# Two gaps between arrays in SBUF resized, and 48 idle products behind the last unit

## The reference

```python
h = layer_norm(x) * (1.0 + sc1) + sh1
proj = h @ w_in
...
mix = merged @ w_out
up = causal_dwconv(h @ w_up, w_dw_f, b_dw_f)
f = (gelu(gt) * v) @ w_down
...
def swiglu(x, w13, w2):
    g, u = split(x @ w13, 2)
    return (silu(g) * u) @ w2
```

## Time and profile before

| what | value |
|---|---|
| median of 3 runs | 1039.6 us (1038.9 to 1039.86) |
| the profiled execution | 1041.34 us, span 1039.5 us |
| PE busy | 1023.4 us (98%), 7499 products |
| DVE, ACT, POOL busy | 73%, 55%, 3% |
| granted TensorE clock, mean | 0.997 |

### The profile page before, as it was taken

One profiled execution on the slowest core, in us unless ns is written; L12 is line 12 of the kernel. 1 busy time (PEld: TensorE's weight loads), 2 busy tenths in 40 slices (PEclk: granted clock), 3 DMA queues, 4 the chain that ended last, 5 costly groups with the idle time before them and its releaser, 6 DMA issues.

```text
span 1039.5 us, 18332 instructions
## 1 busy us (share of the span) xinstructions
PE 1023.4 (98%) x7499; PEld 958.9 (92%) x7499; DVE 754.0 (73%) x1293; ACT 572.9 (55%) x960; POOL 27.5 (3%) x34
## 2 busy tenths in 40 slices
PE   8999999999999999999999999999999999999997
PEld 7999998999999998999987999999899878999996
DVE  6988998899777788877867555555889576555555
ACT  5573447665555586724646445444746565444443
POOL 0000000000100042000000000000000000000000
PEclk9999999999999999999999999999999999999999
DMA  9999873588765533622245555665364426655511
GB/s 370 418 419 370 316 243 124 196 270 274 233 190 193 165 108 115 224 63 80 84 142 186 167 186 191 188 194 186 121 229 158 132 95 250 209 187 183 186 58 41
DMA packets 59603, 201.22 MB, mean 194 GB/s; under 512 B 10496, under 2 KB 10880, under 8 KB 59264
## 3 DMA queue, kind: packets, MB, share of 16 engines
q1 hardware_dynamic: 58368, 199.98, 56.2%
q10 hardware_dynamic: 1152, 0.07, 0.1%
HBM read 198.71 MB, written 1.31 MB: 192 GB/s over the span
## 4 chain that ended last, share of the span: by engine, by line
PE 86%; DVE 10%; ACT 2%; issue 1%; DMA 1%; SPq 0%; DVEq 0%; ACTq 0%
PE ps L632 73%; PE ps L1012 4%; DVE lo L1899 2%; DVE raw L1883 1%; DVE B L2356 1%; PE ps L818 1%; PE ps L720 1%; DVE B L1968 1%; PE ps L771 1%; PE ps L869 1%; DMA B<-in_t 1%; ACT hi L1300 1%; PE ps L806 0%; PE ps L791 0%; DVE sm L2180 0%
## 5 line engine op out<-in xcount | busy, mean ns | idle before, releaser
L1899 DVE TENSOR_TENSOR lo<-raw,hi 128x1024 fp32r<-128x1024 f32 x297 | 360.8, 1222 | 123.3 <-ACT hi L1300 122.6
L632 PE MATMUL ps<-hh,hi 128*128 128x256 f32 x1528 | 432.1, 283 | 2.2 <-DVE hl L1945 1.1
L632 PE MATMUL ps<-hl,hi 128*128 128x256 f32 x1528 | 426.7, 279 | 0.0
L632 PE MATMUL ps<-hh,lo 128*128 128x256 f32 x1528 | 426.7, 279 | 0.0
L1300 ACT ACTIVATE hi<-raw 128x1024 fp32r<-128x1024 f32 x305 | 318.4, 1052 | 50.2 <-PE ps L632 49.1
L632 PEld LDWEIGHTS ps<-hh,hi 128*128 128x128 f32 x1528 | 287.3, 188 | 6.3 <-issue 2.0
L632 PEld LDWEIGHTS ps<-hl,hi 128*128 128x128 f32 x1528 | 287.3, 188 | 1.9 <-issue 0.3
L632 PEld LDWEIGHTS ps<-hh,lo 128*128 128x128 f32 x1528 | 287.3, 188 | 0.0
L632 PE MATMUL ps<-hi,fh 128*128 128x512 f32 x192 | 76.3, 397 | 0.0
L632 PE MATMUL ps<-lo,fh 128*128 128x512 f32 x192 | 75.9, 395 | 0.0
L632 PE MATMUL ps<-hi,fl 128*128 128x512 f32 x192 | 75.8, 395 | 0.0
(11 more groups left out here) (333 smaller groups left out, 1277.4 us busy)
## 6 DMA issues: line engine op xcount, KB each, us to landing
raw<-in_w SPq DMA_DIRECT2D x356, 512.0 KB, 4.3
Z<-in_w SPq DMA_DIRECT2D x9, 512.0 KB, 9.9
B<-in_t SPq DMA_DIRECT2D x2, 512.0 KB, 4.9
B<-in_w SPq DMA_DIRECT2D x2, 512.0 KB, 8.5
h<-in_w SPq DMA_DIRECT2D x2, 512.0 KB, 7.7
xa<-in_x SPq DMA_DIRECT2D x1, 1024.0 KB, 8.6
B<-in_r SPq DMA_DIRECT2D x1, 1024.0 KB, 6.4
out<-h SPq DMA_DIRECT2D x4, 256.0 KB, 2.0
```

The source lines that it names most:

```text
L632: m = g.matmul(o, l, r, start=first and n == 0, stop=last and n == 2, skip_group_check=True)
L1899: g.tensor_tensor(lo[:, j % SPLIT, :], raw[:, PLACE[j] % RAW, :], hi[:, j % SPLIT, :].bitcast(F), ALU.subtract).then_inc(*up("lo", j))
```

## The change

`gap0` has 12 elements instead of 24 (48 bytes instead of 96), `gap1` 20 instead of 8 (80 instead of 32). The sum of the two is the same. In `tensor`, two helpers are defined, and the first is called four times behind the last unit: 4 x 4 x 3 = 48 narrow products into bank 4 that nobody reads, whose moving operand is `hh` or `hl` taken `shift` elements later, and whose stationary operand is slot 0 of `hi` or `lo` taken `by` elements later.

```diff
-        gap0 = sb("gap0", [P, 24])
+        gap0 = sb("gap0", [P, 12])
         hh = sb("hh", [P, NC, S], FR)
         hl = sb("hl", [P, NC, S], FR)
-        gap1 = sb("gap1", [P, 8])
+        gap1 = sb("gap1", [P, 20])
...
         def tensor(g, s):
+            def idle_rows(shift, n, by=0):
+                xh, xl = (x[:, :, :].rearrange("p a b -> p (a b)") for x in (hh, hl))
+                for k in range(n):
+                    a = k * S + shift
+                    w = k % 4 * P + by
+                    three(bank[4][:, 0:S], hi[:, 0, w:w + P], lo[:, 0, w:w + P], xh[:, a:a + S], xl[:, a:a + S], True, True)
+
+            def idle_wide(shift, n, by=0):
+                xh, xl = (x[:, :, :].rearrange("p a b -> p (a b)") for x in (hh, hl))
+                for k in range(n):
+                    a = k * S + shift
+                    three(bank[5][:, :], hi[:, 0, by:by + 512], lo[:, 0, by:by + 512], xh[:, a:a + P], xl[:, a:a + P], True, True,
+                          flip=True)
...
             ffn_tokens("w131", "w21", "w13r1", "x5", x5_free)
+            idle_rows(2, 4)
+            idle_rows(30, 4)
+            idle_rows(1, 4)
+            idle_rows(16, 4, 16)
```

## The result

The changed kernel takes 1056.4 us (median of 4 runs, 1056.38 to 1056.47) against 1039.5 us before (four runs): a ratio of 1.0165, 95% interval [1.0152, 1.0178], slower by 16.9 us. The forecast was 1055 us.

The account below looks back on a forecast made before the run. It took the time from one TensorE product's start to the next as the bound: 1041.3 us profiled + 15.3 = 1056.6, less 1.7 for the median, say 1055 us. Own range 1050 to 1058, with rival A 1025 to 1058.

Parts of the forecast that it names:

- Places: SBUF addresses: rounding to 32 bytes puts hh and hl 32 bytes nearer, not 48, and fh and all behind 32 farther.
- Part 1: 4584 narrow products moving hh or hl: 120 ns apart, the idle products' level, +15.3 us; other bound -15.3 us.
- Part 2: 528 narrow products moving fh or fl: distance 160 stays at 113.3 ns, 0 taken; bound 0 to +1.8 us.
- Part 3: Wide products, 528 over hh or hl and 576 over fh or fl: no change, bound -3.7 to +3.7 us.
- Parts 4 and 5: 48 idle products hidden under last norm and stores, cost 0; all else moved, such as transposes, 0, under +1 us.
- Sum: Whole kernel: profiled 1041.3 + 15.3 = 1056.6 us, less 1.7 for the median: 1054.9, say 1055 us.
- rival A: Operand distances repeat each 64 bytes, so hh and fh products swap levels: -13.5 us, 1026 us; chance 0.30.
- Rival B: Address doesn't matter at this grain; a phase between TensorE's two streams holds a step: 1039.6 us; chance 0.18.

Follow-up runs that it names:

- e4: Kernel before plus, behind the last unit, sets of narrow products at 64 operand distances and wide ones at 16; one execution, 113.0 to 120.0 ns at the kernels' distances.
- e12: Kernel before plus runs of 37 narrow products at 16 operand distances, each behind four different entries; one execution, 113.3 and 117.8 ns at distance 192.
- e3: Kernel before plus only the 48 idle products behind the last unit, nothing moved; 1039.4 us against 1039.6, ratio 0.9998.
- e1: Kernel before with only hh and hl 32 bytes nearer, no idle products; 1055.3 us against 1039.6, ratio 1.0152.
- e9: Kernel before with hh and hl 16 bytes nearer, fh and fl 48 bytes nearer; 1042.0 us against 1037.9, ratio 1.0049.
- e5: Kernel before with hh and hl 32 bytes farther, all else in place; 1045.4 us against 1037.9, ratio 1.0073.
- e2: Kernel before with hh and hl in place, fh and everything behind it 32 bytes farther; 1043.4 us against 1039.6, ratio 1.0035.
- e7: Kernel before with hi and all behind it 32 bytes farther, distances between a product's operands kept; 1039.0 us against 1037.9, ratio 1.0010.
- e10: Kernel before with hh, hl 80 bytes farther, fh, fl 48, all behind 64; narrow distance 144 throughout; 1030.9 us against 1039.1, ratio 0.9918.
- e8: Kernel before plus runs of 48 narrow products at three distances, each behind seven entries; one execution, 113.3 or 117.7 to 117.8 ns at distance 192.

## Why the prediction was right, and where not

- **Places.** 32 bytes nearer and all behind 32 farther, not 48 and in place: right, and it decided. The exact 48 gave +2.7 us.
- **Part 1**, `hh` to the idle products' level: right. 119.8 ns against 120 predicted, +13.8 us against +15.3. The mean over the whole kernel was 116.8 before and 119.8 after, 3.0 ns apart where the sum took the full step from 116.7 to 120. That D = 0 means 120 for other arrays too is shown by e4 (119.6 ns for `hh` over `hh` and for `hi` under `hh`), and that it does behind four different entries by e12.
- **Part 2**, `fh` at D = 160 left at 113.3, bound +1.8 us: wrong, +3.3 us. The step was "by the trend": between D = 144 and 160 there is no trend, 113.3 and 120.0 lie side by side. A bound of one step was too narrow where the highest row was two steps up.
- **Part 3**, wide ones at 0 within -3.7 to +3.7: -2.5 and +0.6 us, inside; that D = 0 is good for wide products was not foreseen.
- **Parts 4 and 5** at nothing: right (e3 0.9998; transposes with `first` 109 ns in the median, before and after).
- **Sum.** The mechanism of part 1 was right. That the products' sum agrees so well is luck: 15.3 predicted, 15.2 by the traces, because the misses of parts 1 to 3 cancel. Missed were the 2.4 us near 397 us, where TensorE waited 1.9 instead of 0.6 us and the clock stood at 0.51; the prediction expected waits to take up 1 to 2 us and not to add any. The stretch is there in the traces of e1 and of e9's slowest run, and not in those of the other moved versions, e5 among them, which is slower than before too. Why the wait grows was not tried. The measured 1056.4 us lie in the forecast's own range of 1050 to 1058; the stated one, 1025 to 1058, was that wide because it took in rival A.
- **Rival A** (modulo 64) fell by e2. **Rival B** was half right: one distance can hold two steps, as the rows of 203.95 to 207.79 us hinted, but only at some distances; 0, 160 and 144 were the same behind every entry. By the rule of the Trainium skill's page "SBUF — State Buffer", section "Who interferes with whom", that "PE and ACT never wait on anyone", the place was to be free. That is not borne out: e7 keeps the distances and comes to 1.0010 of before, e1 and e10 change them and go 1.5% up and 0.8% down with the same instructions. The N / 2.4 + 2.5 ns that the prediction compares with are given by the Trainium skill's page "TensorE: Matmul & The Clock Gate", section "Back-to-back issue gap", for a single matmul by itself, not for a stream with a weight load each; nothing in the sum hung on it. Which part of the engine or the memory holds the products up, the traces don't show.

## What to carry to other kernels

Where products of 256 float32r columns fill the time, the distance of the stationary from the moving operand is worth up to 6% of them (120.0 against 113.3 ns); look at the time from start to start by pair of arrays, and compare pairs before touching anything. Pick a distance that is fast behind different work, not the fastest row of one sweep: D = 192 and 240 measured 113 ns in the sweep and gave nothing or a loss in the kernel, 144 settled at 113.3 ns behind every entry and gave 0.8%. Work out the addresses after the allocator's rounding, and of everything behind the gap too.

## What was not expected of the hardware

- One distance can have two lasting levels: at D = 192, 113.3 or 117.8 ns for runs of 37 to 48 products at least. The level changes with what ran before, but the last 24 products alone don't fix it (e8, e12). `fh`, not moved, went from 113.7 to 117.9 ns when only `hh` moved (e1).
- The dependence is fine: D = 144 gave 113.3 ns, 16 bytes to either side 118.4 to 118.8 (D = 128) and 120.0 (D = 160).
- A distance can need some 15 products to settle: at D = 144 they take 118 ns in the mean behind wide ones, then 113.3 (e10).
- Products with 512 moving columns prefer other distances than those with 256: at D = 0 228 ns instead of 233, where the narrow ones are at 120, the upper end.
